# A local attention phase with three value products per step, value tiles padded with ones and zeros, and every low part of the probabilities on GpSimd

## The reference, cut to what matters

```python
def _mixer_swa(h, positions, w_in, sinks):
    proj = h @ w_in
    q, k, v, z = jnp.split(proj, ...)
    q, k = _rope(q, positions), _rope(k, positions)
    # per block of 128 queries: keys of the block before and of its own
    s = where(mask, einsum('bqgrd,bkgd->bgrqk', q, k) * scale, NEG_INF)
    pr = softmax(concatenate([s, sinks], -1))[..., :-1]
    o = einsum('bgrqk,bkgd->bqgrd', pr, v)
    return o * silu(z)
```

## Time and profile before

| | us |
|---|---|
| median of the runs shown | 3315.48 |
| the profiled execution | 3316.73 |
| its span, first to last instruction | 3314.9 |
| TensorE busy in the span | 3019.1 |
| GpSimd busy in the span | 1289.7 |
| first scoring of `swa` | 519.53 |
| first DMA issue of the phase after it | 842.25 |

### The profile page before, as it was taken

The page is one execution under the profiler, slowest core; times in us unless marked ns, Lnnn a source line. Parts: engine busy times, 40 slices in busy tenths (PEclk is TensorE's granted clock), DMA queues, the critical chain, the costliest instruction groups (busy, mean ns, idle before and its releaser), DMA issues. The chain is left out here.

```text
span 3314.9 us, 41291 instructions
## 1 busy us (share of the span) xinstructions
PE 3019.1 (91%) x13635; PEld 2356.5 (71%) x13660; DVE 1914.6 (58%) x2832; ACT 1578.0 (48%) x2778; POOL 1289.7 (39%) x1108
## 2 busy tenths in 40 slices
PE   8999967888799989999786789999999999799998
PEld 6888865555577777888665567777777777577776
DVE  3544215666367644444464477878787787347753
ACT  3111103556433543444323247777777777534543
POOL 0122003555222232000020058888888888512333
PEclk9999978999999999999897879999999999899999
DMA  5255255774898566554557935243342522498654
GB/s 173 74 121 134 90 130 128 165 162 108 253 268 254 182 212 222 184 178 153 182 224 265 319 78 121 68 101 92 84 109 68 122 71 52 145 280 260 221 201 157
DMA packets 252341, 531.18 MB, mean 160 GB/s; under 512 B 28841, under 2 KB 77097, under 8 KB 243569
## 3 DMA queue, kind: packets, MB, share of 16 engines
q1 hardware_dynamic: 227792, 511.35, 52.4%
q10 hardware_dynamic: 24352, 17.44, 2.2%
HBM read 351.06 MB, written 177.37 MB: 159 GB/s over the span
## 5 line engine op out<-in xcount | busy, mean ns | idle before, releaser
L2161 POOL TENSOR_TENSOR mla_pl<-mla_p,mla_ph 128x512 fp32r<-128x512 f32 (+3 forms) x640 | 706.9, 1120 | 365.2 <-ACT mla_p L2026 356.6
L1347 PE MATMUL end_bank<-end_xh,end_whi 128*128 128x512 f32 x1600 | 640.7, 400 | 79.5 <-DVE end_wlo L1502 44.5
L1348 PE MATMUL end_bank<-end_xl,end_whi 128*128 128x512 f32 x1600 | 630.2, 394 | 0.0
L1349 PE MATMUL end_bank<-end_xh,end_wlo 128*128 128x512 f32 x1600 | 629.8, 394 | 0.0
L1887 PE MATMUL mla_score<-mla_q,mla_k 96*128 96x512 f32 (+7 forms) x1920 | 554.9, 391 | 6.9 <-DMA mla_q<-mla_m_t 6.9
L1389 ACT CAST end_whi<-end_wraw 128x1024 fp32r<-128x1024 f32 x188 | 197.0, 1048 | 565.1 <-PE end_bank L1349 329.7
L1502 DVE TENSOR_TENSOR end_wlo<-end_wraw,end_whi 128x1024 fp32r<-128x1024 f32 x188 | 233.5, 1242 | 386.6 <-ACT end_whi L1389 386.2
L2025 ACT ACTIVATE mla_ph<-mla_score 128x512 fp32r<-128x512 f32 (+3 forms) x640 | 340.9, 533 | 225.8 <-PE mla_score L1887 222.1
L1887 PEld LDWEIGHTS mla_score<-mla_q,mla_k 96*128 96x128 f32 (+1 forms) x1920 | 361.9, 192 | 93.2 <-issue 37.4
L2055 DVE TENSOR_REDUCE mla_mx<-mla_mx 128x1 f32<-128x512 f32 (+3 forms) x640 | 372.0, 603 | 93.9 <-PE mla_mx L1887 93.3
L1347 PEld LDWEIGHTS end_bank<-end_xh,end_whi 128*128 128x128 f32 x1600 | 304.9, 191 | 164.1 <-DVE end_wlo L1502 59.8
(11 more groups left out here) (236 smaller groups left out, 4847.4 us busy)
## 6 DMA issues: line engine op xcount, KB each, us to landing
end_wraw<-in_w_out SPq DMA_DIRECT2D x64, 512.0 KB, 8.1
end_wraw<-in_pe_gate SPq DMA_DIRECT2D x64, 512.0 KB, 5.0
end_wraw<-in_w_in SPq DMA_DIRECT2D x56, 512.0 KB, 3.9
swa_q<-scratch_q_hi SPq DMA_DIRECT2D x32, 512.0 KB, 12.5
scratch_proj<-end_out_f SPq DMA_DIRECT2D x64, 256.0 KB, 7.2
end_raw<-scratch_o SPq DMA_DIRECT2D x32, 512.0 KB, 11.1
end_factor<-scratch_inv SPq DMA_DIRECT2D x64, 256.0 KB, 9.4
scratch_sum<-end_out_f SPq DMA_DIRECT2D x64, 256.0 KB, 5.4
```

The costliest lines, as they stand in the source:

```text
L1347: nc.tensor.matmul(bank, wh[:, at], xh[:, k0 + k, :], start=(k == 0), stop=False)
L1348: nc.tensor.matmul(bank, wh[:, at], xl[:, k0 + k, :], start=False, stop=False)
L1349: last = nc.tensor.matmul(bank, wl[:, at], xh[:, k0 + k, :], start=False, stop=(k == kc - 1))
L2161: pool.tensor_tensor(p_lo[b][:, off:TC], prob[b][:, off:TC], p_hi[b][:, off:TC].bitcast(F32), ALU.subtract).then_inc(p_lo_ok, 1)
```

## The change

The value tile now comes in two: `swa_v` has the high part in columns 0 to 63 and ones in columns 64 to 127, `swa_vl` the low part and zeros. The ones and zeros are written once for each buffer by VectorE at the start of the phase. Three products per step, `swa_v` by `swa_ph`, `swa_vl` by `swa_ph` and `swa_v` by `swa_pl`, fill `swa_o`: rows 0 to 63 are the whole result and row 64 is the denominator. `swa_den`, `swa_ones`, `low_half` and `finish` are gone in `swa`. All 124 low parts are GpSimd's, the gate product is VectorE's and reads `swa_o` in PSUM, the row of denominators is copied by ScalarE. The two PSUM banks of `swa_den` go to a second buffer for the maxima's items. The store of a chunk moves one step earlier in ScalarE's order. The values are loaded by two DMAs, each of which takes 256 bytes out of every 512 of the source. In both attention phases the wait for `p_lo_ok` now stands before the product with the low part, behind the products with the high part.

```diff
-        den_lag, store_lag = (lag + 3, lag + 5) if long else (lag + 1, lag + 4)
+        den_lag, store_lag = (lag + 3, lag + 5) if long else (lag, lag + 3)
...
+        vals_lo = None if long else [s.sb(f"vl{b}", [P, vb, P], F32R) for b in range(2)]
...
-        mx_ps = [s.ps(f"mx{b}", [P, mx_w]) for b in range(2 * TC // mx_w)]
+        mx_ps = [s.ps(f"mx{b}", [P, mx_w]) for b in range(2)]
...
         def on_vector(g):
-            return not long and not flat[g][2]["last"]
+            return False
...
             def weigh(g):
                 u, k, st = flat[g]
                 c, off = chunk_of[g], st["off"]
+                pe.wait_ge(probs, g + 1)
+                if st["first"] and c >= 2:
+                    pe.wait_ge(row_ok, c - 1)
+                    if not long:
+                        pe.wait_ge(gated, c - 1)
+                v = vals[u % 2][:, st["v"], :]
+                out, high, low = o_ps[c % 2][:, off:TC], p_hi[g % nbuf][:, off:TC], p_lo[g % nbuf][:, off:TC]
+                mm(out, v, high, st["first"], False)
+                if not long:
+                    mm(out, vals_lo[u % 2][:, st["v"], :], high, False, False)
                 if on_vector(g):
                     pe.wait_ge(p_lo_v_ok, low_count[g])
                 else:
                     pe.wait_ge(p_lo_ok, low_count[g])
-                if st["first"] and c >= 2:
-                    pe.wait_ge(row_ok, c - 1)
-                    if not long:
-                        pe.wait_ge(sum_ok, c - 1)
-                v = vals[u % 2][:, st["v"], :]
-                high, low = p_hi[g % nbuf][:, off:TC], p_lo[g % nbuf][:, off:TC]
-                mm(o_ps[c % 2][:, off:TC], v, high, st["first"], False)
-                last = mm(o_ps[c % 2][:, off:TC], v, low, False, st["last"])
-                if not long:
-                    mm(den_ps[c % 2][:, off:TC], ones[:], high, st["first"], False)
-                    last = mm(den_ps[c % 2][:, off:TC], ones[:], low, False, st["last"])
-                last.then_inc(weighed, 1)
+                mm(out, v, low, False, st["last"]).then_inc(weighed, 1)
...
-            def denominators(c):
+            def out_gate(c):
                 dve.wait_ge(weighed, last_of[c] + 1)
+                dve.wait_ge(gate_in[c % small], 16 * (c // small + 1))
                 if c >= small:
-                    dve.wait_ge(den_stored[c % small], 16 * (c // small))
-                vec.tensor_copy(den_row[c % small][:], den_ps[c % 2][0:1, :]).then_inc(row_ok, 1)
+                    dve.wait_ge(stored[c % small], 16 * (c // small))
+                vec.tensor_tensor(o_out[c % small][:], o_ps[c % 2][0:HEAD_DIM, :], gate[c % small][:], ALU.mult
+                                  ).then_inc(gated, 1)
...
-        yield vals[:, 0:n // P, :], v[g, :, t0 // P:(t0 + n) // P]
+        for tile, at in ((vals, 0), (vals_lo, HEAD_DIM)):
+            yield tile[:, 0:n // P, 0:HEAD_DIM], v[g, :, t0 // P:(t0 + n) // P, at:at + HEAD_DIM]
```

More of the change, by code:

```diff
@@ L1736, in attention_phase @@
         m_t = s.sb("m_t", [blocks, P], F32R)
-        o_low = [s.sb(f"o_low{b}", [HEAD_DIM, TC]) for b in range(2)]
-        o_sum = [s.sb(f"o_sum{b}", [HEAD_DIM, TC]) for b in range(2)]
+        if long:
+            o_low = [s.sb(f"o_low{b}", [HEAD_DIM, TC]) for b in range(2)]
+            o_sum = [s.sb(f"o_sum{b}", [HEAD_DIM, TC]) for b in range(2)]
         den_row = [s.sb(f"den_row{b}", [1, TC]) for b in range(small)]
@@ L1854, in load_low @@
                     sp.wait_ge(scores, ends[u - 2])
-                for n, (dst, src) in enumerate(cfg["load_b"](u, q_tiles[1][u % 2], k_tiles[1][u % 2], vals[u % 2])):
-                    if n == cfg["n_load_b"] - 1 and u >= 2:
+                v_tiles = [vals[u % 2]] if long else [vals[u % 2], vals_lo[u % 2]]
+                for n, (dst, src) in enumerate(cfg["load_b"](u, q_tiles[1][u % 2], k_tiles[1][u % 2], *v_tiles)):
+                    if n == cfg["n_load_b"] - len(v_tiles) and u >= 2:
                         sp.wait_ge(weighed, ends[u - 2])
@@ L2001, in denominators @@
             def denominators(c):
-                act.wait_ge(den_ok, c + 1)
+                if long:
+                    act.wait_ge(den_ok, c + 1)
+                else:
+                    act.wait_ge(weighed, last_of[c] + 1)
                 if c >= small:
                     act.wait_ge(den_stored[c % small], 16 * (c // small))
-                act.copy(den_row[c % small][:], den_ps[c % 2][0:1, :]).then_inc(row_ok, 1)
+                at = 0 if long else HEAD_DIM
+                act.copy(den_row[c % small][:], o_ps[c % 2][at:at + 1, :]).then_inc(row_ok, 1)
             def store(c):
@@ L2032, in _ @@
                         max_row(u + 1)
-                if g - lag - 1 in closes:
+                if long and g - lag - 1 in closes:
                     low_half(closes[g - lag - 1])
-                if long and g - den_lag - 1 in closes:
+                if g - den_lag - 1 in closes:
                     denominators(closes[g - den_lag - 1])
@@ L2044, in _ @@
                 op = vec.memset(tile[rows:kr, :].bitcast(F32), 1.0)
-            if not long:
-                op = vec.memset(ones[:].bitcast(F32), 1.0)
+            for b in range(0 if long else 2):
+                vec.memset(vals[b][:, :, HEAD_DIM:P].bitcast(F32), 1.0)
+                op = vec.memset(vals_lo[b][:, :, HEAD_DIM:P].bitcast(F32), 0.0)
             op.then_inc(const_ok, 1)
@@ L2139, in _ @@
                             negate(u + 1)
-                if not long and g - den_lag in closes:
-                    denominators(closes[g - den_lag])
-                if g - lag - 1 in closes:
+                if not long and g - lag - 1 in closes:
+                    out_gate(closes[g - lag - 1])
+                if long and g - lag - 1 in closes:
                     finish(closes[g - lag - 1])
@@ L2162, in _ @@
                                        ALU.subtract).then_inc(p_lo_ok, 1)
-                if g - lag - 2 in closes:
+                if long and g - lag - 2 in closes:
                     out_gate(closes[g - lag - 2])
```

9 lines of the change are left out of this document (3 added, 6 removed).

## The result

The changed kernel takes **3273.02 us** (median of four runs, 3269.31 to 3278.85) against 3314.18 us of the kernel before (3306.72 to 3318.55): a ratio of 0.9877, 95% interval 0.9856 to 0.9899. It is faster by 41 us where I forecast 17, and it lies under my range. The profiled execution took 3278.85 us with a span of 3277.0, which is 37.9 less than before.

A forecast was written before the change was run, and what follows sets the result against it. The gate's DMA behind each burst bounds the loops (B), TensorE the stretches A and C. A -7.5, B +4.0, C -13.7 and `mla` 0 make -17.2 us: 3298, forecast 3291 to 3306, wider range 3276 to 3315.

The forecast's parts named there:

- A: `swa` from first scoring (519.53) to the first burst's issue (565.87), 46.3 us, bound by TensorE; forecast -7.5 us.
- C: `swa` from the last burst's issue (770.97) to the next phase's first DMA issue, 71.3 us, TensorE-bound; forecast -13.7 us.
- The waits for the reduce in A and C: TensorE's waits for the reduce, 3.1 us in A and 3.0 in C, both go with the second maxima buffer.
- The end of a chunk in A: From last weighing to `gated`, one VectorE instruction and GpSimd's product go: A 1.9 us shorter.
- The products: One of seven per step goes, 0.233 us each, 124 times, 28.9 us of TensorE's time: 3.0 in A, 7.7 in C.
- B: Five loops between A and C, 205.1 us, bound by the gate's DMA behind each burst; forecast +4.0, five times 0.8.
- R: Way from the gate's arrival to the next burst's issue in each loop of B; forecast 15.9 us, as before.
- The low parts: All 124 on GpSimd at 1.28 us a step against TensorE's 1.40; +1.5 us charged for jitter in C.
- `mla`: The latent attention keeps its products, and its moved wait for the low part costs nothing: 0, bounds -2 and +3 us.
- TensorE as the bound throughout: Rival: B gains too, from removed products and late low parts, 52 us in all, 3264; chance 0.12.
- The packet prices: Rivals on 256-byte pieces in the burst: half rate, 3307, chance 0.15; 60 ns or more a piece, 3325, chance 0.11.
- the direct wait: Rival: the first weighing's new wait for the gate product costs three us more in each loop, 3313; chance 0.12.

## Why the prediction was wrong, by its steps

- **Where the stretches began.** The step that failed is the first: I looked at `swa` from the first scoring on. I priced the second maxima buffer by TensorE's waits in A and C and left out the prologue, where the same edit has nothing to hide behind. That is 14.7 of the 25.0 us between forecast and result (of the 21.7 that the phase gave beyond the forecast), and taking the buffer away gave 14.0 back.
- **The waits for the reduce in A and C**, -3.1 and -3.0: oversized. They did go, but bringing them back cost 0.5 and 1.2. In A the changed kernel has a wait of 1.0 in their place, behind a gate product whose gate was loaded after the prologue's loads.
- **The end of a chunk in A**, -1.9: it was -4.1. Before, 6.2 us passed from the start of chunk 6's last weighing (559.67) to the burst's issue (565.87), after 2.15 (536.76 to 538.91). I had counted the instructions and not that GpSimd took a low part first. GpSimd before, then VectorE after:

```profile
562.71 1.29 POOL L2161 TENSOR_TENSOR swa_pl<-swa_p,swa_ph 128x512 fp32r<-128x512 f32 x1 [0.34 <-ACT swa_p L2026]
563.96 1.27 POOL L2152 TENSOR_TENSOR swa_o_out<-swa_o_sum,swa_gate 64x512 f32<-64x512 f32 x1
```
```profile
537.59 0.67 DVE L2126 TENSOR_TENSOR swa_o_out<-swa_o,swa_gate 64x512 f32<-64x512 f32 x1
```

- **The products.** 0.233 each is what they take, but not what they are worth: 12 in A returned 0.6 and 33 in C 6.2, not 3.0 and 7.7 (the 0.6 is one reading in the stretch that repeats worst). In the loops most of their 18.2 us was taken up by the stall, as forecast: 4.5 came back.
- **B**, +4.0 forecast, +2.6 measured: right in both parts. The burst grew by 0.5 and not 0.8; R stayed at 15.9. That R meets the forecast to a tenth is luck: it is 16.2 and 15.3 in the two versions with one buffer in the loops, which are the same there. It is also a sum of parts that do not stay by themselves: R grew by 1.5 with the early wait, and by 0.9 with a fourth product and 0.6 with shared low parts, of which the last is inside that scatter.
- **The low parts**, +1.5 in C for GpSimd's pace: not seen. TensorE waits 0.7 us for a low part in C, and sharing the low parts again made C 0.7 longer, not shorter. The moved wait is part of this: in front of the step's first product it costs 11.8 us in the phase. I had given it no term in `swa`; that was a price at nothing without a reason.
- **C**, -13.7 forecast, -16.1 measured. Undone one at a time, the edits return 6.2, 2.2, 1.2 and 0.7. The other 5.8 must be the shorter end of a chunk, for which I had 5.1 + 1.3 - 1.9; it was not undone by itself, so this is argued. In A the same sum gives 0.6, 1.2, 0.5 and 2.6 undone and 4.1 at the end of the chunk, 9.0 of 10.8.
- **`mla`**, 0: it is 2.6 us longer between its scorings in one profile. Versions with the same `mla` lie between 914.3 and 918.4, so this is within the scatter.
- **The rivals.** TensorE as the bound throughout would have given 3264, near the measured time, and is still refuted: the loops did not gain (B +2.6), and they fell by 8 us each only when the gates were issued ahead, and by 10 with more output buffers. The packet prices (12 ns more for a packet) and the direct wait (R 15.9) did not come either. A number near a rival's doesn't make the rival right; the stages have to agree.

## What to carry to other kernels

Cut the whole phase that an edit touches, from its first load on, and price the edit in each stretch apart: a second buffer that saves little where other work fills the wait can save more than half of the time where a unit's first items run alone (3.50 to 1.28 us an item). A wait behind a burst of loads isn't shortened by less work; issue the small transfers that are needed soon ahead of the burst, and look then which buffer (here the stores') is late next. And when an engine's pace is within a tenth of the step (here 1.28 against 1.40), move the wait for it as far back in the step as the data allow.

## What the runs showed of the hardware

- TensorE's granted clock went with its waits in these versions, and this added to two effects. With 1.3 us of wait behind each item it stayed at 1.2 GHz for the whole prologue (0.50, twice measured); without the waits it rose within the items. In the loops a stall of some 8 us a loop went with a granted clock of 0.88, with 30.2 instead of 41.1 us of it the clock was 0.93, and without it 1.00.
- The issue of the second value tile holds SyncE's queue. SyncE's timeline of the changed kernel, the two value tiles of a burst, and the second one of the last burst:

```profile
547.10 0.54 SPq L1858 DMA_DIRECT2D swa_v<-scratch_v  x1
547.68 7.00 SPq L1858 DMA_DIRECT2D swa_vl<-scratch_v  x1
...
749.50 0.87 SPq L1858 DMA_DIRECT2D swa_vl<-scratch_v  x1
```

  The issue of a DMA of the same size takes 0.54 us or 7.00 (5.9 to 10.2 in the five loops, 5.7 and 17.9 in the prologue). In the last burst, which has fewer loads ahead of it, it takes 0.87; that what is queued ahead sets it is my reading and not tested. Without the second tile (the version with rows of 512 bytes) the gate came only 0.9 us earlier, so little of those 6 to 10 us reaches the loop.
